# One decoder layer on one core: the order of the attention pairs, feature-turned normed rows, and residual products right behind each norm

## The chip, the cores and the metric

The kernel runs on one core of one Trainium2 chip. The metric is the device time of one execution, in microseconds (us). TensorE (PE) multiplies, VectorE (DVE), ScalarE (ACT) and GpSimd (POOL) do the rest; SyncE (SP), ScalarE and GpSimd also issue DMA transfers. All values are float32. A matmul with float32 operands shows as two records in the trace, so "x8" in a row is four matmuls.

## What is computed

One layer with a prompt of 256 tokens (two tiles of 128) and 8 sample tokens, D = 1024. Shortened:

```python
u, cB, cC, q, k, v, qi, ki, wi, qm, g = split(x @ w_in)     # one projection, 6216 columns
# branch A: short gated convolution; branch C: 4 heads over 256 memory tokens
# branch B: 8 heads; an indexer scores keys, each query keeps k of them
sc  = sum_h relu(qi_h . ki) * wi_h          # prompt: top 64 of 256; samples: top 256 of 2049
p   = softmax(q . k[chosen]);  out = p @ v[chosen]    # samples gather k, v rows from a paged cache
m   = g0*(convA @ w_a) + g1*(attn @ w_b) + g2*(mem @ w_c)
h   = LN(alpha*x + m @ w_o)
# router: best of 4 groups, best 2 of its 8 experts; 32 experts, each 1024 -> 2x256 -> 1024
y   = sum_e gate[:, e] * (silu(a_e) * b_e) @ w_down[e],   a_e, b_e = h @ w_up[e]
out = LN(alpha*h + y)
```

The expert weights are 32 x 3 MiB, read once.

## The kernel before, in words

Each engine has one instruction list, written by hand, with semaphores between them. There is no planner: the order of the source is the order on each engine.

**Start and projections** (PE `chunk`, L563 on). `x` is turned, then `w_in` comes in 1 MB units through four slots. ScalarE issues the loads of the constants (L1327, L1329). A bisection over the sample scores runs beside the gate tiles (`gate_tile`, 24 tiles of 4 x 128 columns of `w_in`, eight matmuls each).

**Attention** (PE L813 to L920). Twelve heads in six pairs: pairs 0 and 1 are memory heads, 2 to 5 are prompt heads. For pair p, `scores(p)` writes two PSUM banks; `softmax(n)` on VectorE scales (and masks) a head's scores into SBUF and takes the row maxima; `exps(n)` on ScalarE; `inverse(n)` on VectorE; `normalise(n)` on ScalarE; `turn(n)` on TensorE turns the probabilities; `values(p)` multiplies them with the values; `head_out(p)` on VectorE copies the result out. Gate tiles stand between these as other work for TensorE. VectorE also has the indexer sums (L2101) and 16 rounds that find the 64 largest scores (`topk_round`, L2055); prompt heads need all of them.

**Samples' keys and values.** When the 256 positions per sample are known (`idx_ready`, L2045), GpSimd issues 16 gathers of key rows (L1632), at most two of them open, then 16 gathers of value rows (L1648), four per pair. Key products are shared out: 12 on GpSimd into four buffers (L1645), each summed on VectorE (`key_sum`, L1845), 5 wholly on VectorE (`key_dot`: L1686 and L1855). Softmax and value product of the samples are interleaved with the branch tiles (`branch_tile`, L895) and their `merge` on VectorE (L2091). SyncE loads `w_o` into the keys' place when all key products are summed (L447), and the first expert weights when the sample values are done (`sa_p`, 9 of them).

**First norm and router** (PE L940 to L1045, DVE L2204 to L2345). `wo_first`, `wo_second` are the output projection (L946, L965). Tile 0, the samples, then tile 1: `residual`, `ln_stats`, `ln_centre` (into `ytmp`), `ln_rstd`, `ln_scale` (into `h3`, `h_ready`). The router's logits come from the un-normed rows. `wo_ps` 4 marks the end of the output projection. `residual_tile(t)` multiplies `h3` by alpha and opens the PSUM banks in which the experts' output is added (L1008, L1012).

**Experts** (PE L1025 to L1260). A token's slot in an expert is a one-hot column of `Ssl`; a gather is a matmul with `h3[:, t, k::KT]` as weights (128 features k, k+8, ...) and `Ssl` moving: `first_part` (L1028), `first_gather` (L1060), `second_gather` (L1079), `gather` (L1097). Eight quads of four experts; SyncE streams their weights in 2 MB units through nine places (`p` counts them), waiting for `used_w` from p = 9 on. Expert 0's lower half comes aside (`down_0`, `down_1`).

## Time and profile before

| | |
|---|---|
| median of 3 runs | 612.38 us (610.49 to 614.92) |
| the profiled execution | 612.95 us, its span 611.1 us |
| PE busy | 551.1 us (90%) |
| PEld busy | 348.4 us (57%) |
| DVE busy | 277.9 us (45%) |
| ACT, POOL busy | 101.1 us, 63.9 us |
| mean granted TensorE clock | 0.954 |
| HBM read | 160.14 MB, 267 GB/s over the span |

The span is the time from the first to the last instruction; the profiled execution's own time is 1.85 us longer. Shares are means over stages with different limits: each stage has to be read by itself, in stretches of time and in the order of each engine.

### The profile page before, as it was taken

How to read it: one execution, taken by the hardware profiler on the slowest of the kernel's cores; microseconds unless marked ns; L12 is line 12 of the kernel's file. 1: busy time of each engine (PE TensorE's matmuls, PEld its weight loads, DVE VectorE, ACT ScalarE, POOL GpSimd, SP SyncE). 2: the span in 40 equal slices, each digit the busy share in tenths (PEclk: the TensorE clock that was granted, in tenths of full speed). 3: DMA queues.
4: the chain of work that ended last, by engine and by line, in shares of the span. 5: the costliest groups of instructions: out<-in, count | busy, mean ns of one | idle time of the engine just before them, and what ended most of it. 6: DMA issues, size and time to landing. Idle time of an engine off the chain costs nothing.

```text
span 611.1 us, 8674 instructions
## 1 busy us (share of the span) xinstructions
PE 551.1 (90%) x3518; PEld 348.4 (57%) x3518; DVE 277.9 (45%) x766; ACT 101.1 (17%) x243; POOL 63.9 (10%) x70
## 2 busy tenths in 40 slices
PE   7999999999999995999799899999999995987671
PEld 4556566475688773777576456766654661522120
DVE  1273765666677687759862496312010200100026
ACT  1001111011310123545100211011101110101011
POOL 0000000000200034587200000000000000000002
PEclk9999999998999996999899997999999999897796
DMA  8981231944443445576869926899999999999971
GB/s 294 372 321 45 93 138 50 365 140 140 131 132 120 139 138 189 175 242 190 330 247 403 321 70 262 306 417 388 424 390 422 420 419 420 422 419 421 417 302 71
DMA packets 47886, 163.53 MB, mean 268 GB/s; under 512 B 5954, under 2 KB 22812, under 8 KB 35812
## 3 DMA queue, kind: packets, MB, share of 16 engines
q1 hardware_dynamic: 39280, 139.81, 59.4%
q0 software_dynamic: 3472, 14.31, 6.9%
q10 hardware_dynamic: 5092, 8.83, 4.0%
q8 instruction: 29, 0.48, 0.3%
q14 instruction: 13, 0.11, 0.1%
HBM read 160.14 MB, written 2.77 MB: 267 GB/s over the span
## 4 chain that ended last, share of the span: by engine, by line
PE 57%; DMA 17%; DVE 17%; ACTq 5%; issue 2%; ACT 1%; SPq 0%; POOLq 0%; POOL 0%; DVEq 0%
PE bank L578 11%; DMA ring<-in_w_down 10%; PE bank L769 10%; PE bank L1122 6%; DMA ring<-in_w_up 5%; PE bank L539 4%; PE bank L1214 2%; PE bank L965 2%; ACTq L1476 2%; PE bank L624 2%; ACTq L1475 2%; DVE ring L1686 2%; PE bank L1079 2%; PE bank L1097 2%; PE bank L592 2%
## 5 line engine op out<-in xcount | busy, mean ns | idle before, releaser
L769 PE MATMUL bank<-work,ring 128*128 128x264 f32 x384 | 94.1, 396 | 0.0
L578 PE MATMUL bank<-ring,work 128*128 128x512 f32 (+2 forms) x224 | 90.6, 544 | 2.1 <-DMA ring<-in_w_in 2.1
L769 PEld LDWEIGHTS bank<-work,ring 128*128 128x128 f32 x384 | 71.2, 192 | 14.8 <-issue 2.8
L1122 PE MATMUL bank<-ring,work 128*32 128x512 f32 x304 | 52.4, 665 | 14.2 <-DMA ring<-in_w_up 11.0
L578 PEld LDWEIGHTS bank<-ring,work 128*128 128x128 f32 x224 | 40.0, 190 | 32.8 <-issue 29.7
L2350 DVE SCALAR_TENSOR_TENSOR work<-work,bank 128x256 f32<-128x256 f32 x8 | 3.4, 422 | 87.0 <-ACT work L1530 87.0
L2362 DVE COPY gates<-bank 128x512 f32<-128x512 f32 x8 | 5.5, 692 | 74.7 <-PE bank L1214 67.7
L895 PE MATMUL bank<-work,ring 128*128 128x264 f32 x128 | 32.6, 400 | 4.3 <-DVE gates L2091 4.3
L1122 PEld LDWEIGHTS bank<-ring,work 128*32 128x32 f32 x304 | 13.9, 121 | 37.5 <-issue 37.4
L1122 PE MATMUL bank<-proj,work 128*32 128x512 f32 x128 | 30.6, 622 | 2.3 <-DMA ring<-in_w_up 1.9
L895 PEld LDWEIGHTS bank<-work,ring 128*128 128x128 f32 x128 | 24.0, 195 | 12.5 <-DVE gates L2091 5.1
L1214 PE MATMUL bank<-ring,work 128*32 128x512 f32 x176 | 27.0, 635 | 2.8 <-DMA ring<-in_w_down 2.1
L1665 POOL TENSOR_TENSOR proj<-proj,ring 128x512 f32<-128x512 f32 x1 | 1.3, 1268 | 255.6 <-ACT proj L1577 255.6
L1157 PE MATMUL bank<-gates,work 128*128 128x512 f32 x56 | 25.4, 596 | 0.0
L1097 PE MATMUL bank<-gates 128*128 128x256 f32 x96 | 24.4, 411 | 0.0
L1351 ACT ACTIVATE work<-bank 128x512 f32<-128x512 f32 x16 | 9.6, 597 | 87.2 <-PE bank L539 87.2
L1097 PEld LDWEIGHTS bank<-gates 128*128 128x128 f32 x96 | 23.2, 335 | 0.1
L1779 DVE SCALAR_TENSOR_TENSOR work<-bank,work 128x512 f32<-128x512 f32 x16 | 11.1, 692 | 25.3 <-PE bank L624 25.2
L1632 POOL DMA_INDIRECT ring<-in_cache_k,idx x16 | 15.3, 955 | 68.4 <-DVE idx L2045 51.6
L1394 ACT ACTIVATE gates<-bank,gates 128x264 f32<-128x264 f32 x24 | 11.5, 480 | 65.1 <-PE bank L769 60.1
L539 PE MATMUL bank<-cst,proj 128*128 128x128 f32 (+1 forms) x80 | 14.5, 304 | 7.5 <-ACT proj L1433 6.9
L624 PEld LDWEIGHTS bank<-work 128*128 128x128 f32 x128 | 16.4, 191 | 8.2 <-issue 8.2
(337 smaller groups left out, 845.1 us busy)
## 6 DMA issues: line engine op xcount, KB each, us to landing
ring<-in_w_up SPq DMA_DIRECT2D x19, 2048.0 KB, 19.8
ring<-in_w_down SPq DMA_DIRECT2D x13, 2048.0 KB, 24.3
ring<-in_w_in SPq DMA_DIRECT2D x22, 1024.0 KB, 5.9
proj<-in_w_up SPq DMA_DIRECT2D x8, 2048.0 KB, 20.7
misc<-in_w_up SPq DMA_DIRECT2D x5, 1024.0 KB, 25.9
gates<-in_w_up SPq DMA_DIRECT2D x5, 1024.0 KB, 20.2
ring<-in_w_o SPq DMA_DIRECT2D x4, 1024.0 KB, 8.7
proj<-in_w_down SPq DMA_DIRECT2D x2, 2048.0 KB, 24.3
```

The costliest lines, as they stand in the source:

```text
L539: return nc.tensor.transpose(out, in_, ident[0:n, 0:n])
L578: last = mm(bank[2 * (i % 2) + t][:, 0:w], lhs[:, k, 128 * t:128 * t + 128], rhs[:, k % 4, :], start=(k == 0), stop=(k == KT - 1))
L592: last = mm(bank[4 + i % 2][32 * j:32 * j + 32, 0:w // 4], lhs[:, k, 256:288], rhs[:, k % 4, j * w // 4:(j + 1) * w // 4], start=(k == 0), ...
L624: last = mm(bank[6][:, 128 * i:128 * i + 128], kt4[g % 2][:, 128 * i:128 * i + 128], QB, start=True, stop=True)
L769: last = mm(b[:, 0:TOK], w[:, k, 128 * (n % 2):128 * (n % 2) + 128], xT[:, k, 0:TOK], start=(k == 0), stop=(k == KT - 1))
L895: last = mm(b[:, 0:TOK], w2[:, k % 2, 128 * n:128 * n + 128], brT[:, k0 + k, 0:TOK], start=(k == 0), stop=(k == nk - 1))
L965: last = mm(bank[2 + dh][:, :], mT[k][:, 128:256], wo(k)[:, 512 * dh:512 * dh + 512], start=(k == 0), stop=(k == 6))
L1097: last = mm(bank[6 + i][:, PC * kk:PC * kk + PC], h3[:, t, k::KT], Ssl[:, t, :], start=(t == 0), stop=(t == 2))
L1122: last = mm(bank[5][32 * j:32 * j + 32, :], xTe[q // 2 % 2][:, k, s0:s0 + CAP], up_of(n + j // 2, j % 2, r), start=(k == 0), stop=(k == KT ...
L1157: mm(bank[2 * t + dh][:, :], GT[q % 2][:, 128 * t:128 * t + 128], Ysb[:, 512 * dh:512 * dh + 512], start=False, stop=False)
L1214: last = mm(bank[6 + dh][32 * j:32 * j + 32, :], hT2[:, f, 32 * j:32 * j + 32], wd, start=(f == 0), stop=(f == 1))
L1632: pool.indirect_dma_start(Kg[:, i, :], None, ck, bass.IndirectOffsetOnAxis(ap=idx_sb[:, i:i + 1], axis=0))\
```

## The change

- **Start**: the big load of constants is issued after the first weight unit has landed, and behind ScalarE's copies of the turned `x`.
- **Pairs**: `scores(0)` and its maxima move ahead of the compaction; memory heads take maxima and exponentials straight from PSUM; `scores(p+1)` stands between the two turns of pair p; all indexer sums stand ahead of the first top-k round; `head_out` moves from VectorE to ScalarE.
- **Samples**: gathers are issued without a limit; all 17 key products are on GpSimd, in place, with the value gathers between and behind them; VectorE sums 4, 4, 5, 3 and 1 rows at a time.
- **Norm**: `ln_scale` stays in `ytmp`; ScalarE copies tile 0 and the samples into `hturn`, which stores a row's features as k x 128 + q for feature 8q + k; tile 1 is written there by VectorE (`ln_scale_turned`), and normed once more into `ytmp`. The residual products read `ytmp` right behind each norm. Gathers load `h3[:, t, 128k:128k+128]`.
- **Stream**: `down_0[1]` waits for `route_ready` two units later, and the count of the fullest expert is taken in bank 5.

```diff
-TOPK_ROUNDS = ((8, 10, 14), (14, 16, 16), ...
+TOPK_ROUNDS = ((0, 3, 8, 11), (11, 16, 16, 16), (16, 16, 16, 16), ...
+KEY_SUMS = ((), (), ((0, 4),), ((4, 8),), ((8, 13),), ((13, 16), (16, 17)))
+        hturn = gate_t[:, 0:3072].rearrange("p (t k q) -> p t q k", t=3, k=KT)
@@ sync
-                    sp.wait_ge(kd_mul, NPROD)
-                    sp.wait_ge(kd_dot, NDOT)
+                    sp.wait_ge(kd_sum, NSUMS)
-                if p == NWS:
+                if p == NWS + 2:
                     sp.wait_ge(route_ready, 1)
@@ tensor
+                elif p == 2:
+                    pe.wait_ge(at_e, 4 * p)
...
             index_scores(0)
+            scores(0)
             gate_tile(11)
...
             for p in range(PAIRS_H):
                 turn(2 * p)
-                turn(2 * p + 1)
                 if p + 1 < PAIRS_H:
                     scores(p + 1)
                 if p == 0:
                     gate_tile(14, part=1)
+                turn(2 * p + 1)
...
-            wo_second(0, (0, 1, 2, 3, 4, 5, 7, 6)).then_inc(wo_ps, 1)
+            wo_second(0, (0, 1, 2, 3, 4))
+            pe.wait_ge(h_ready, 1)
+            pe.wait_ge(aid_ready, 1)
+            residual_tile(0).then_inc(res_ps, 1)
+            wo_second(0, (5, 7, 6)).then_inc(wo_ps, 1)
...
             wo_second(1, range(4))
+            pe.wait_ge(h_ready, 2)
+            residual_samples().then_inc(res_ps, 1)
...
-                        last = mm(bank[6 + b][:, 128 * kk:128 * kk + 128], h3[:, t, 4 * b + kk::KT], Ssl[:, t, 0:128],
+                        last = mm(bank[6 + b][:, 128 * kk:128 * kk + 128], h3[:, t, 128 * (4 * b + kk):128 * (4 * b + kk) + 128], Ssl[:, t, 0:128],
@@ scalar
-            act.wait_ge(x2_in, 16)
-            act.dma_start(cst[:, 128:nconst], a["consts"][:, 128:nconst]).then_inc(cst_in, 16)
...
+            act.wait_ge(unit_sem(0), UC[0])
+            act.dma_start(cst[:, 128:nconst], a["consts"][:, 128:nconst]).then_inc(cst_in, 16)
...
+            def h_copied(n, t, m):
+                act.wait_ge(h_ready, n)
+                act.activation(hturn[0:m, t], ytmp[0:m, :].rearrange("p (q k) -> p q k", k=KT), ACT.Copy).then_inc(hp_ready, 1)
@@ gpsimd
+            for i in range(16):
+                key_gather(i)
+            pool.wait_ge(sa_p, 4)
+            value_gather(0)
+            value_gather(1)
+            pool.wait_ge(qr_sb, 1)
+            pool.wait_ge(knew_in, 32)
+            pool.wait_ge(kg_in, 16 * 16)
+            for i in range(17):
+                key_product(i)
+                if i % 2 == 1 and 2 + i // 2 < 9:
+                    value_gather(2 + i // 2)
+            for i in range(9, 16):
+                value_gather(i)
@@ vector
+            def key_sum(i0, i1):
+                dve.wait_ge(kd_mul, i1)
...
                     inverse(2 * p + 2)
                     if p == PAIRS_H - 2:
                         for i0, i1 in KEY_SUMS[p]:
                             key_sum(i0, i1)
                     inverse(2 * p + 3)
...
+            merge(2)
+            for i0, i1 in KEY_SUMS[PAIRS_H - 1]:
+                key_sum(i0, i1)
+            merge(3)
             sample_max(H, 17, sbias)
...
+            dve.wait_ge(hp_ready, 1)
+            dve.wait_ge(res_ps, 1)
             ln_centre(h3, 2, lng, ytmp)
...
+            ln_scale_turned(ytmp, 1, lnb, hp_ready)
```

TensorE at the head of the pair loop, before: the two turns of pair 0 stand together, ahead of the next scores and of a gate tile and a half.

```order
L769 MATMUL bank<-work,ring 128x264 x8
L539 MATMUL bank<-cst,proj 128x128 x8
L828 MATMUL bank<-misc 128x256 x4
L769 MATMUL bank<-work,ring 128x264 x12
L873 MATMUL bank<-proj 64x256 x4
L769 MATMUL bank<-work,ring 128x264 x8
L539 MATMUL bank<-cst,proj 128x128 x8
L828 MATMUL bank<-work 128x128 x2
```

The same place in the change (L535 are turns, L826 scores, L765 gate tiles, L871 values).

```order
L765 MATMUL bank<-work,ring 128x264 x8
L535 MATMUL bank<-cst,proj 128x128 x4
L826 MATMUL bank<-misc 128x256 x4
L765 MATMUL bank<-work,ring 128x264 x4
L535 MATMUL bank<-cst,proj 128x128 x4
L765 MATMUL bank<-work,ring 128x264 x8
L871 MATMUL bank<-proj 64x256 x4
L765 MATMUL bank<-work,ring 128x264 x8
L535 MATMUL bank<-cst,proj 128x128 x4
L826 MATMUL bank<-work 128x128 x2
```

The second turn now has the next pair's scores and half a gate tile ahead of it, and the scores of pair 2 (L826 from `work`) come between the turns of pair 1.

VectorE from the softmax of the last pair to the first merges (L2091), before: L1845 sums a GpSimd product, L1686 with L1855 are products made on VectorE.

```order
L2073 TENSOR_REDUCE misc<-proj 128x1 x2
L1845 TENSOR_REDUCE gates<-misc 128x8
L2079 RECIPROCAL misc<-misc 128x2
L1845 TENSOR_REDUCE gates<-misc 128x8
L2079 RECIPROCAL misc<-misc 128x2
L1845 TENSOR_REDUCE gates<-proj 128x8
L2085 COPY work<-bank 128x256
L1686 TENSOR_TENSOR ring<-ring,proj 128x512
L1855 TENSOR_REDUCE gates<-ring 128x8
L1686 TENSOR_TENSOR proj<-proj 128x512
L1855 TENSOR_REDUCE gates<-proj 128x8
L2091 SCALAR_TENSOR_TENSOR gates<-gates,bank 128x264 x2
```

The change (L2056 and L2059 softmax, L2065 inverse, L1864 sums over several rows, L2097 merge).

```order
L2056 SCALAR_TENSOR_TENSOR proj<-bank,proj 128x384
L2059 TENSOR_REDUCE misc<-proj 128x1 x2
L2056 SCALAR_TENSOR_TENSOR proj<-bank,proj 128x384
L2059 TENSOR_REDUCE misc<-proj 128x1 x2
L2065 RECIPROCAL misc<-misc 128x2
L1864 TENSOR_REDUCE gates<-ring 128x40
L2065 RECIPROCAL misc<-misc 128x2
L2097 SCALAR_TENSOR_TENSOR gates<-gates,bank 128x264 x3
L1864 TENSOR_REDUCE gates<-ring 128x24
L1864 TENSOR_REDUCE gates<-proj 128x8
L2097 SCALAR_TENSOR_TENSOR gates<-gates,bank 128x264
```

No product is left on VectorE; a sum over five rows (128x40) stands between the two inverses, and sums over three and one row behind the third merge.

TensorE in the output projection of tile 1 (L965 `wo_second`, L977 logits, L999 to L1001 slot counts), before.

```order
L965 MATMUL bank<-ring,gates 128x512 x8
L539 MATMUL bank<-cst,gates 128x8 x8
L989 MATMUL bank<-misc,cst 128x72
L977 MATMUL bank<-proj,work 128x36 x8
L977 MATMUL bank<-proj,work 8x36 x8
L965 MATMUL bank<-ring,gates 128x512 x4
L539 MATMUL bank<-cst,gates 128x128 x4
L965 MATMUL bank<-ring,gates 128x512 x3
L999 MATMUL bank<-proj,cst 128x32
L1000 MATMUL bank<-proj,cst 128x32
L1001 MATMUL bank<-proj,cst 128x32
L965 MATMUL bank<-ring,gates 128x512
```

The change (L963 `wo_second`, L980 and L985 the residual products of tile 0 and of the samples, L975 logits).

```order
L963 MATMUL bank<-ring,gates 128x512 x5
L980 MATMUL bank<-gates,cst 128x512 x2
L963 MATMUL bank<-ring,gates 128x512 x3
L535 MATMUL bank<-cst,gates 128x8 x8
L1003 MATMUL bank<-misc,cst 128x72
L975 MATMUL bank<-proj,work 128x36 x8
L975 MATMUL bank<-proj,work 8x36 x8
L963 MATMUL bank<-ring,gates 128x512 x4
L985 MATMUL bank<-gates,cst 32x256 x4
L535 MATMUL bank<-cst,gates 128x128 x4
```

Both residual products now stand inside the output projection, ahead of its last matmuls and so ahead of `wo_ps` 4.

## Rows read from the trace of the kernel before

**Rows 1.** The chain that ended last, end of the weight stream: start us, us, what.
```profile
527.20 63.45 DMA ring<-in_w_down x2
```

**Rows 2.** SyncE's queue in order of time: start us, us, line, operation.
```profile
311.72 0.88 SPq L471 DMA_DIRECT2D ring<-in_w_up  x2
...
370.83 0.88 SPq L471 DMA_DIRECT2D ring<-in_w_up  x2
...
394.94 0.89 SPq L471 DMA_DIRECT2D ring<-in_w_down  x2
```

**Rows 3.** Stretches: us, busy PE PEld DVE ACT POOL, PEclk, DMA share, GB/s.
```profile
235.00:237.50 2.50, 1.12 (x4) 0.72 (x4) 1.74 (x8) 1.76 (x4) 1.47 (x2) 0.50 0.21 59
...
375.00:377.50 2.50, 2.50 (x5) 1.18 (x5) 1.85 (x11) 0.00 (x0) 0.00 (x0) 0.50 1.02 423
...
390.00:392.50 2.50, 2.50 (x22) 1.64 (x25) 0.50 (x4) 0.60 (x1) 0.00 (x0) 1.00 0.52 216
...
392.50:395.00 2.50, 2.50 (x28) 0.78 (x24) 0.00 (x0) 0.00 (x0) 0.00 (x0) 1.00 0.64 210
...
395.00:397.50 2.50, 2.50 (x28) 0.78 (x24) 0.00 (x0) 0.00 (x0) 0.00 (x0) 1.00 0.62 141
...
450.00:455.00 5.00, 5.00 (x52) 1.43 (x44) 0.00 (x0) 0.00 (x0) 0.00 (x0) 1.00 0.90 324
```

**Rows 4.** TensorE in order of time, attention pairs and branch tiles.
```profile
223.32 1.03 PE L828 MATMUL bank<-misc 64*128 64x256 f32 x8
...
236.08 1.12 PE L539 MATMUL bank<-cst,proj 128*128 128x128 f32 x4 [4.93 <-ACT proj L1433]
...
239.18 1.11 PE L539 MATMUL bank<-cst,proj 128*128 128x128 f32 x4 [1.98 <-ACT proj L1433]
...
240.22 2.08 PE L828 MATMUL bank<-misc 64*128 64x256 f32 x8
...
242.23 6.62 PE L769 MATMUL bank<-work,ring 128*128 128x264 f32 x24
...
283.37 0.82 PE L539 MATMUL bank<-cst,proj 128*128 128x128 f32 x6
...
295.73 2.12 PE L895 MATMUL bank<-work,ring 128*128 128x264 f32 x4 [4.14 <-DVE gates L2091]
...
307.75 3.70 PE L730 MATMUL bank<-ring,work 128*32 128x128 f32 x128 [0.78 <-DVE gates L1686]
```

**Rows 5.** VectorE in order of time, the last two pairs.
```profile
285.28 0.56 DVE L2070 SCALAR_TENSOR_TENSOR proj<-bank,proj 128x384 f32<-128x384 f32 x1
...
291.04 2.01 DVE L1686 TENSOR_TENSOR ring<-ring,proj 128x512 f32<-128x512 f32 x1
...
293.08 0.69 DVE L1855 TENSOR_REDUCE gates<-ring 128x8 f32<-128x512 f32 x1
...
293.80 0.69 DVE L1686 TENSOR_TENSOR proj<-proj 128x512 f32<-128x512 f32 x1
```

**Rows 6.** GpSimd in order of time, gathers and a key product.
```profile
219.77 1.02 POOL L1632 DMA_INDIRECT ring<-in_cache_k,idx  x1 [51.60 <-DVE idx L2045]
...
221.10 0.97 POOL L1632 DMA_INDIRECT ring<-in_cache_k,idx  x1 [0.30 <-issue]
...
250.96 0.95 POOL L1632 DMA_INDIRECT ring<-in_cache_k,idx  x1 [2.01 <-DMA ring<-in_cache_k,idx]
...
285.37 1.28 POOL L1645 TENSOR_TENSOR proj<-ring,proj 128x512 f32<-128x512 f32 x1
```

**Rows 7.** ScalarE in order of time, a plain copy (with a scale).
```profile
341.40 1.91 ACT L1479 ACTIVATE work<-work 128x2048 f32<-128x2048 f32 x1 [38.45 <-issue]
```

**Rows 8.** TensorE in order of time, first slot gather.
```profile
378.58 3.88 PE L1028 MATMUL bank<-gates 128*128 128x128 f32 x16
```

**Rows 9.** By line: weight loads, rows stride 8 words (L1028), adjacent (L1157), min/median/max ns.
```profile
L1028 PEld LDWEIGHTS bank<-gates x48: 312/336/338, 377.7 to 390.2; 128*128 128x128 f32 x48
...
L1157 PEld LDWEIGHTS bank<-gates,work x56: 186/190/208, 428.0 to 579.2; 128*128 128x128 f32 x56
```

**Rows 10.** Start: TensorE's first chunk, ScalarE's constants load.
```profile
10.44 13.97 PE L578 MATMUL bank<-ring,work 128*128 128x512 f32 x32 [2.10 <-DMA ring<-in_w_in]
...
6.57 0.35 ACTq L1329 DMA_DIRECT2D cst<-in_consts  x1
```

More of the change, by code:

```diff
@@ L341, in layer @@
         knew_in, vg_in, xres_in, ln_in = (sem(n) for n in ("knew_in", "vg_in", "xres_in", "ln_in"))
-        kg_in = [sem(f"kg_in{i}") for i in range(2)]
+        kg_in = sem("kg_in")
         ln2_in, lnv_in = sem("ln2_in"), sem("lnv_in")
@@ L978, in logits, with residual_tile, residual_samples @@
                 return last
+            def residual_tile(t):
+                for dh in range(2):
+                    last = mm(bank[2 * t + dh][:, :], alpha_id, ytmp[:, 512 * dh:512 * dh + 512], start=True, stop=False)
+                return last
+            def residual_samples():
+                for j in range(4):
+                    last = mm(bank[4][32 * j:32 * j + 32, 0:256], alpha_id[0:NS, 0:32],
+                              ytmp[0:NS, 256 * j:256 * j + 256], start=True, stop=False)
+                return last
             pe.wait_ge(r_ready, 1)
@@ L1035, in _ @@
             mm(bank[5][:, 64:96], ones[:, 0:128], mask[:, 0:32], start=False, stop=False)
-            mm(bank[5][:, 64:96], ones[:, 0:128], mask[:, 64:96], start=False, stop=True).then_inc(pos_ps, 1)
-            first_part(1, range(4), (0, 2))
+            mm(bank[5][:, 64:96], ones[:, 0:128], mask[:, 64:96], start=False, stop=True)
+            for t in range(3):
+                last = mm(bank[5][:, 96:128], ones[:, 0:128], mask[:, 32 * t:32 * t + 32], start=(t == 0), stop=(t == 2))
+            last.then_inc(pos_ps, 1)
+            pe.wait_ge(hp_ready, 3)
             pe.wait_ge(first_s, 2)
-            pe.wait_ge(h_ready, 3)
             for b in range(2):
                 first_part(b, range(4), (1,)).then_inc(first_ps, 1)
-            for t in range(3):
-                last = mm(bank[3][:, 0:32], ones[:, 0:128], mask[:, 32 * t:32 * t + 32], start=(t == 0), stop=(t == 2))
-            last.then_inc(cnt2_ps, 1)
+            pe.wait_ge(cnt_read, 1)
             def first_gather(i):
@@ L1223, in _ @@
                 up_half(0, b)
+            pe.wait_ge(h_ready, 3)
+            residual_tile(1)
             gate_turn(0)
@@ L1649, in value_gather, with key_product @@
                                         bass.IndirectOffsetOnAxis(ap=idx_sb[:, i:i + 1], axis=0)).then_inc(vg_in, 16)
-            for p in range(1, PAIRS_H - 1):
-                pool.wait_ge(at_t, 2 * p + 1)
-                products, gathers = list(KEY_PRODUCTS[p]), list(VALUE_GATHERS[p])
-                for i in range(4):
-                    value_gather(gathers[i])
-                    if i < len(products):
-                        key_product(products[i])
+            def key_product(i):
+                row = Kg[:, i, :] if i < 16 else knew
+                pool.tensor_tensor(row, row, qrep, ALU.mult).then_inc(kd_mul, 1)
+            for i in range(16):
[12 more added lines that the diff above has]
+                value_gather(i)
             pool.wait_ge(m_ready, KT)
@@ L2096, in _ @@
                 w = 128 * (t + 1)
-                for r in range(*INDEX_ROUNDS[i]):
-                    topk_round(r)
                 dve.wait_ge(is_act, i + 1)
```

275 lines of the change are left out of this document (119 added, 156 removed).

## The prediction, made before the change was run

> **What bounds the kernel now.** I read the page's slices first: TensorE is near 100% busy up to 500 us, the DMA engines are full from 400 us to 590 us. Two limits follow each other, so the chain of waits comes next. Its last long piece is a weight load of the experts that ends at 590.65 us [rows 1], 20 us before the end, and from there on nothing in the change touches the work. So the question is when the weight stream ends. SyncE's queue says what starts it: the first expert weights leave at 311.72 us, behind the samples' values; the places of `w_o` are refilled at 370.83 us, behind `wo_ps` 4; the first place freed by the experts is refilled at 394.94 us [rows 2]. The stretches show how full it is: between 390 and 397.5 us it moved 216, 210 and 141 GB/s instead of about 420, and 324 GB/s at 450 to 455 us [rows 3]. A microsecond counts if it brings 311.72 forward, or `wo_ps` 4 after it, or fills one of those holes. Speed on TensorE behind 400 us counts only through the holes.
>
> Up to 311 us the bound is TensorE, so I looked in its order of time for idle time with a releaser. It waits 4.93 and 1.98 us for normalised probabilities before the two turns of pair 0, and 4.14 us before the third branch tile, for VectorE's first merge [rows 4]. Behind the first two it also runs at the lower of its two clocks: the granted clock is 0.50 at 235 us, 1.2 GHz [rows 3], and scores that took 1.03 us take 2.08 [rows 4].
>
> **The parts and their cost.** *Start.* TensorE waits 2.10 us for the first weight unit, until 10.44 us; the constants' load is issued at 6.57 us and shares the engines with it [rows 10]. Behind the unit instead, it gives back about half of the wait, as two transfers share: -1.1 us (ends 0 and -2.1). The constants are needed only by the first rotary step, after the 13.97 us chunk.
>
> *Pairs 0 and 1.* The normalised probabilities of head 0 now exist before the compaction ends, since its scores, maxima and exponentials stand ahead of it and the copy through VectorE is gone. Turn 0 follows the gate tiles at once. Turn 1 has the next scores and half a tile ahead of it. VectorE then has the indexer sums, 3 top-k rounds, two maxima, 5 rounds, and the inverses: by the same durations as before I get the inverses at 240 us and the turns of pair 1 at 243.4 us, so ScalarE is ready 1 to 2 us early. Both idle times go, 6.9 us. The lower clock goes with them: it cost 0.56 us on each turn (four records in 1.12), 1.05 on the scores, and about 0.9 on the tiles (24 records in 6.62 us, [rows 4]; 5.7 at full speed): 3.0 us. Sum -9.9 us; turn 4 then stands at 253.7 us, where I find `normalise(4)` ready at 253.7: no slack. The other end is that one wait of 4.93 us comes back with its half-speed work: -4.
>
> *Samples.* VectorE loses its 5 products, of which one took 2.01 us, and sums 17 rows at 0.69 us each instead [rows 5]. GpSimd: idle until 219.77 us, then 16 gathers at 1.33 us each, the distance of the two that waited for nothing [rows 6]; all keys there by about 245; 17 products of 1.28 us with 7 value gathers of 1.0 between them, until 277; 7 more gathers until 286.5; landed at 290. The samples' values are due on TensorE at 294.6. Covered, by 4 us. The other end for a gather is 2.08 us, (250.96 - 219.77) / 15, when two are open at most [rows 6]; I take 1.33 since nothing waits now, and keep the other as a rival.
>
> *Branch tiles.* From turn 8 (283.37 us, [rows 4]) to the load that waits for the samples' values (311.72, [rows 2]) were 28.3 us. In the new order: merge 0 at 7.9 us after turn 8 (the five-row sum, 3.4 us, stands before it), branch tile 2 at 8.4, sums of four rows 2.8 us, merge 3 at 13.2, then sample steps and merges by turns, probabilities ready at 20.9, values until 24.9. So -3.4 us. The ends are -5.8 (idle 4.14 and about 1.7 at half speed behind it, nothing new added) and 0. The first expert weights then leave 13.3 us earlier, or 14.4 with the start. The full stretch that follows keeps its length: both what it carries and what waits for it move together.
>
> *Norm.* The residual products of tile 0 (4 records of 512 columns, 0.44 us each by [rows 10], 32 records in 13.97) and of the samples (8 records of 256 columns, at most the 1.03 us of the scores, [rows 4]) now stand before `wo_ps` 4: +2.7 us. No wait is added to it: tile 0 is scaled 1 us before TensorE comes to its product, the samples 5 us before. VectorE waits for ScalarE's turned copy: 1024 elements, 0.96 us by the plain copy of 2048 [rows 7], and 3.7 us are there. Writing with a stride could cost more; up to 3 times it is hidden. The Trainium skill, SBUF — State Buffer, Door 1, says that each access that crosses into another 16-byte line pays a penalty; these writes all do, reads of weights no longer. By that rule ScalarE's and VectorE's turned writes would be slow too; the sum stays, as the cover above holds.
>
> *Gathers.* A weight load with stride 8 words takes 336 ns, an adjacent one 190 [rows 9]. A first gather record took 3.88 / 16 = 0.24 us [rows 8]; adjacent ones of 128 columns should take about 0.14, as the turns do at full speed (6 in 0.82 us, [rows 4]): 48 records give 5 to 6 us. So TensorE frees the first weight places about 6 us earlier relative to the norm, even at the lower clock that stands there (0.50 at 375 us, [rows 3]). But the loads started by `wo_ps` 4 are 7.9 MB, 18.7 us at 420 GB/s: they fill the engines until 21.4 us after the old `wo_ps` 4. The hole is closed, not more. It is worth (204 + 210 + 279) GB/s x 2.5 us = 1.7 MB, 4.1 us, and the dip at 450 us another 96 x 5 = 0.5 MB, 1.1 us [rows 3]: -5.2 us. The rest of the gathers' gain is idle time of TensorE. `down_0[1]` now queues behind two units, so TensorE waits some 6 us before the first `down`; the next refill needed from it is issued 6 us before the stream would run dry.
>
> **Sum.** -1.1 - 9.9 - 3.4 + 2.7 - 5.2 = -16.9 us. Against the profiled execution, 612.95 us, that is 596.0 us. The median of the runs is 0.6 us lower than that execution; I leave that in the range. All good ends together give -20.3 (592.7).
>
> **Rivals.** (1) *The pairs stay bound by VectorE and ScalarE.* `exps`, gate outputs, `normalise` and now `head_out` are one list on ScalarE, and turn 4 has no slack. For: the zero margin. Against: the later pairs showed none of these waits. One old wait back: -4 instead of -9.9, 602 us. Chance 0.12. (2) *Gathers run at 2.08 us.* Then keys are there at 257, products end at 289, the last value rows land at 305 instead of before 294.6: 10.8 us come back, 607 us. For: two open gathers did not go faster, and weight loads share the engines. Against: each waited for a landing. Chance 0.08. (3) *The hole moves instead of closing*: `h_ready` 3 comes behind the count and the slots, its 2 MB unit leaves late, or TensorE's wait for `down_0[1]` reaches the stream. 5.2 us lost, 601 us. Chance 0.13. (4) *Slower: GpSimd's products hold VectorE.* Place: 245 to 277 us, where top-k, softmax and sums now run beside 17 products. A VectorE product beside one took 2.01 us instead of 0.69 [rows 5], 1.32 more, about a GpSimd product of 1.28 [rows 6]. If every product held a VectorE step on the path, 17 x 1.32 = 22.4 us: 618 us; it ends slower than before from 13 such holds on. Against: the softmax step that ran beside a product took its usual 0.56 [rows 5]. The Trainium skill, SBUF — State Buffer, Who interferes with whom, has VectorE steps with two SBUF inputs shut out by GpSimd steps that read SBUF; by it, only the mask step of the top-k is left to be held, 1.3 us. Chance 0.03. (5) *The layout does nothing*, since the stream hides it: then the 5.2 us are at stake again; its chance is in (3)'s.
>
> **How the numbers follow.** Forecast 0.64, between 590 and 600 (592.7 at the good ends, and 3 us on either side for what a walk through four stages may miss); (1) 0.12, (2) 0.08, (3) 0.13, (4) 0.03. The range of 8 in 10 goes from 589, the forecast's lower edge against the median, to 605: it takes in (1) and (3) and leaves (2) and (4) out. A measurement of this kernel tells about 1% (6 us) from no change, so faster means under 606.3: all but (2) and (4), 0.89, and half of (2), which stands on that edge, less 0.03 for two rivals together: 0.90. Within 1%: 0.07. Slower: 0.03.
>
> **What would show it.** Right: no idle time before turns 0 to 5 and a clock of 1.00 from 230 to 250 us; the wait before branch tile 2 under 1 us; the first expert weights at 297 us; `wo_ps` 4 about 12 us earlier than before; DMA above 400 GB/s from there to the end of the stream, which ends at 574 us; LDWEIGHTS of the gathers at 190 ns. Wrong: TensorE waiting for ScalarE at a turn (1); a gap before the samples' values with GpSimd or a DMA as releaser (2); a hole in the DMA share 15 to 25 us behind `wo_ps` 4 (3); VectorE steps of 1.3 us more beside L1659 products (4).

## The result, and the profile after

The changed kernel took 619.39 us (median of 4 runs, 617.20 to 621.76) beside 611.43 us for the kernel before (4 runs, 609.91 to 614.92): ratio 1.0123, 95% interval 1.0064 to 1.0182. The forecast was 596.0 us, 589 to 605, so it missed by 23 us and on the wrong side. The profiled run took 617.2 us, its span is 615.3 us.

Where it went is seen in SyncE's queue, in order of time. These rows answer [rows 2].

```profile
315.48 1.03 SPq L467 DMA_DIRECT2D ring<-in_w_up  x2
...
377.11 0.88 SPq L467 DMA_DIRECT2D ring<-in_w_up  x2
...
393.24 0.89 SPq L467 DMA_DIRECT2D ring<-in_w_down  x2
```

The first expert weights leave 3.8 us later than before, not 14 us earlier. So 18.2 of the 21.2 us by which the profiled run missed the forecast lie ahead of 315 us. TensorE in order of time, for [rows 4] (`<-issue` marks idle time for which the profile shows no releaser, `<-remote` one that it cannot name):

```profile
228.68 0.60 PE L535 MATMUL bank<-cst,proj 128*128 128x128 f32 x4
232.27 1.83 PE L826 MATMUL bank<-misc 64*128 64x256 f32 x8 [2.99 <-issue]
...
236.86 0.60 PE L535 MATMUL bank<-cst,proj 128*128 128x128 f32 x4
...
241.12 0.48 PE L765 MATMUL bank<-work,ring 128*128 128x264 f32 x1 [1.03 <-issue]
...
243.93 3.68 PE L765 MATMUL bank<-work,ring 128*128 128x264 f32 x8 [1.72 <-issue]
...
256.63 1.12 PE L535 MATMUL bank<-cst,proj 128*128 128x128 f32 x4 [3.28 <-ACT proj L1437]
...
271.32 0.55 PE L535 MATMUL bank<-cst,proj 128*128 128x128 f32 x3 [2.80 <-ACT proj L1437]
...
290.94 0.49 PE L535 MATMUL bank<-cst,proj 128*128 128x128 f32 x3
```

Turns 0 and 1 (228.68, 236.86) come earlier than before (236.08, 239.18), and without their old waits. Then gate tile 15 crawls: single matmuls with 1 to 2 us of nothing between them, though the code has no wait inside a tile. A late report cannot explain these gaps, since nothing is waited for there. Turn 2 was forecast at 243.4 us and stands at 256.63, turn 4 at 253.7 and stands at 271.32, and turn 8 is at 290.94 where 283.37 - 1.1 - 9.9 = 272.4 was expected. VectorE and, below it, ScalarE in the same stretch:

```profile
227.66 1.01 DVE L2105 SCALAR_TENSOR_TENSOR proj<-misc,proj 128x256 f32<-128x256 f32 x2 [2.53 <-issue]
232.31 1.01 DVE L2105 SCALAR_TENSOR_TENSOR proj<-misc,proj 128x256 f32<-128x256 f32 x2 [3.65 <-issue]
...
245.50 0.69 DVE L2050 TENSOR_REDUCE misc<-bank 128x2 f32<-128x512 f32 x1 [10.03 <-remote]
```

```profile
231.25 0.48 ACT L1399 ACTIVATE gates<-bank,gates 128x264 f32<-128x264 f32 x1 [2.90 <-remote]
...
244.05 0.60 ACT L1465 ACTIVATE proj<-bank 128x512 f32<-128x512 f32 x1 [11.84 <-remote]
```

The maxima at 245.50 need only the scores that TensorE ended at 234.1, and ScalarE's copy at 244.05 only the transposes that it ended at 229.3. So what TensorE reported reached the others 11 and 15 us late, while what ScalarE reported to TensorE arrived at once (its copy ended at 232.21, the scores above began at 232.27). Below, such idle time in front of an input that was ready is called a stop. GpSimd alone did not stop; it was letting out key gathers, one per 1.25 us, for [rows 6]:

```profile
219.67 0.97 POOL L1650 DMA_INDIRECT ring<-in_cache_k,idx  x1 [0.31 <-issue]
220.94 1.02 POOL L1650 DMA_INDIRECT ring<-in_cache_k,idx  x1 [0.30 <-issue]
...
240.17 0.95 POOL L1654 DMA_INDIRECT ring<-in_cache_v,idx  x1 [0.30 <-issue]
241.43 2.48 POOL L1659 TENSOR_TENSOR ring<-ring,proj 128x512 f32<-128x512 f32 x2 [0.32 <-DMA ring<-in_cache_k,idx]
```

The last line needs all sixteen keys. The last of them was let out at 237.67 us, so it was reported as landed within 3.8 us: what the gathers told GpSimd was not late.

The stretches 220 to 250 us (busy time of PE, PEld, DVE, ACT, POOL; granted clock; DMA share; GB/s) give the time lost and the lower clock that followed:

```profile
220.00:230.00 10.00, 9.28 (x49) 6.77 (x47) 5.16 (x13) 4.54 (x12) 7.57 (x8) 1.00 0.75 223
230.00:240.00 10.00, 6.69 (x26) 4.63 (x26) 2.92 (x11) 0.97 (x2) 7.72 (x8) 0.83 0.92 307
240.00:250.00 10.00, 7.01 (x21) 4.05 (x21) 4.40 (x4) 2.58 (x7) 9.16 (x9) 0.66 0.45 125
```

The next two stages did what was forecast. Turn 8 to the samples' load took 24.5 us (24.9 forecast), and from there to `wo_ps` 4 61.6 us against 59.1 before, +2.5 (+2.7 forecast). From there to the end of the last long load of the chain ([rows 1]) it took 216.1 us against 219.8, -3.7 (-5.2 forecast); that load ends at 593.23 us:

```profile
529.84 63.39 DMA ring<-in_w_down x2
```

### The profile page after: what moved, and what is told of

Its sections match the earlier page's. It is cut to its first block, busy times and chain, and to the rows that moved or that the text cites. A ratio compares the mean times of both kernels' runs of the same rounds, so it can differ in the third digit from the quotient of the medians.

```text
span 615.3 us, 8656 instructions
## 1 busy us (share of the span) xinstructions
PE 538.8 (88%) x3518; PEld 328.8 (53%) x3518; DVE 271.1 (44%) x740; ACT 106.6 (17%) x251; POOL 68.6 (11%) x75
## 4 chain that ended last, share of the span: by engine, by line
PE 51%; DMA 20%; DVE 17%; ACTq 5%; issue 3%; another core or an unknown queue 2%; ACT 1%; SPq 1%; POOLq 0%; POOL 0%; DVEq 0%
PE bank L574 11%; DMA ring<-in_w_down 10%; PE bank L765 10%; PE bank L1127 5%; DMA ring<-in_w_up 5%; PE bank L535 3%; PE bank L1219 3%; DMA proj<-in_w_down 3%; ACTq L1490 2%; PE bank L963 2%; PE bank L620 2%; ACTq L1489 2%; PE bank L588 2%; PE bank L1102 2%; PE bank L1084 2%
## 5 line engine op out<-in xcount | busy, mean ns | idle before, releaser
L765 PE MATMUL bank<-work,ring 128*128 128x264 f32 x384 | 96.4, 400 | 4.0 <-issue 4.0
L765 PEld LDWEIGHTS bank<-work,ring 128*128 128x128 f32 x384 | 72.0, 195 | 19.4 <-issue 8.1
L1127 PE MATMUL bank<-ring,work 128*32 128x512 f32 x304 | 51.3, 650 | 15.0 <-DMA ring<-in_w_up 10.9
L1219 PE MATMUL bank<-ring,work 128*32 128x512 f32 x176 | 30.0, 672 | 2.8 <-DMA ring<-in_w_down 2.1
L893 PE MATMUL bank<-work,ring 128*128 128x264 f32 x128 | 31.8, 392 | 0.5 <-DVE gates L2097 0.5
L1102 PE MATMUL bank<-gates 128*128 128x256 f32 x96 | 21.8, 383 | 0.0
L1399 ACT ACTIVATE gates<-bank,gates 128x264 f32<-128x264 f32 x24 | 11.5, 478 | 54.8 <-PE bank L765 51.8
L620 PEld LDWEIGHTS bank<-work 128*128 128x128 f32 x128 | 16.4, 191 | 8.2 <-issue 8.2
L535 PE MATMUL bank<-cst,proj 128*128 128x128 f32 (+1 forms) x80 | 14.5, 293 | 6.7 <-ACT proj L1437 6.1
L1659 POOL TENSOR_TENSOR ring<-ring,proj 128x512 f32<-128x512 f32 x16 | 20.0, 1276 | 0.4 <-DMA ring<-in_cache_k,idx 0.3
## 6 DMA issues: line engine op xcount, KB each, us to landing
gates<-in_w_up SPq DMA_DIRECT2D x5, 1024.0 KB, 21.2
```

The source lines that it names most:

```text
L535: return nc.tensor.transpose(out, in_, ident[0:n, 0:n])
L620: last = mm(bank[6][:, 128 * i:128 * i + 128], kt4[g % 2][:, 128 * i:128 * i + 128], QB, start=True, stop=True)
L765: last = mm(b[:, 0:TOK], w[:, k, 128 * (n % 2):128 * (n % 2) + 128], xT[:, k, 0:TOK], start=(k == 0), stop=(k == KT - 1))
L893: last = mm(b[:, 0:TOK], w2[:, k % 2, 128 * n:128 * n + 128], brT[:, k0 + k, 0:TOK], start=(k == 0), stop=(k == nk - 1))
L1102: last = mm(bank[6 + i][:, PC * kk:PC * kk + PC], h3[:, t, 128 * k:128 * k + 128], Ssl[:, t, :], start=(t == 0), stop=(t == 2))
L1127: last = mm(bank[5][32 * j:32 * j + 32, :], xTe[q // 2 % 2][:, k, s0:s0 + CAP], up_of(n + j // 2, j % 2, r), start=(k == 0), stop=(k == KT ...
```

## The experiments

A count is used beside the rows: how often the trace shows a transfer raising its semaphore. A complete trace of this program has 2,798 such updates. The changed kernel's first trace had 2,490, and from 220 to 246 us only 99 updates of any kind, where the kernel before had 271; but that trace of the kernel before lacked 70 transfer updates too (2,728), without a stop. Where all updates are in the trace and nothing stops, a chip is called prompt, and choking where the engines stop. Runs were made on five chips (e1 to e4, e5 to e8, e9 to e12, e13 to e16, e17 to e19); each time below stands beside the kernel before on the same chip. e3, the change without its key gathers, gave no time.

**e1 and e2: how many gathers are open.** A gather is open from its issue to its landing. Key gathers of the change let out two at a time (the cut shown), and those of the kernel before let out without a limit.

```diff
+                if i >= 2:
+                    pool.wait_ge(kg_in[i % 2], 16 * (i // 2))
                 pool.indirect_dma_start(Kg[:, i, :], ...)
```

> The changed kernel, with the key gathers let out as before the change: at most two open at a time. Theory A (sixteen open gathers hold back the loading of the engines' next instructions, so that VectorE, ScalarE and TensorE stop between 225 and 245 us): the three stops of VectorE (2.5, 3.7 and 10.0 us) go, turn 8 moves from 290.94 to about 273 us; but the keys are then there at 257 us, the products end at 289 and the last value rows land at 305, so the gap before the samples' values gives about 10 us back: 603 to 608 us. Theory B (VectorE's steps are held by GpSimd's products beside them): no gain, since the products run as before and only later: 617 us or more. Theory C (the new order of the pairs leaves VectorE and ScalarE no room in itself): the stops stay where they are, 615 to 620 us.

> The kernel before with this one edit: its sixteen key gathers are let out at once. Theory A: VectorE, ScalarE and TensorE stop for 10 us or more between 225 and 245 us, as in the changed kernel, and it gets slower by about 10 us: 618 to 625 us. Theories B and C: nothing but the gathers changes, the products come at the same places, so 611 us as before, or a little less.

Measured: e1 611.76 us, ratio 0.998 (0.995 to 1.002), outside what any of the three theories gave; e2 611.84 us, ratio 0.999 (0.995 to 1.003). e1 has no stop, and loses to late values what it gains, the wait before the samples' values being

```profile
303.04 5.59 PE L726 MATMUL bank<-ring,work 128*32 128x128 f32 x128 [5.40 <-DMA ring<-in_cache_v,idx]
```

e2 lets out its gathers without a limit and has no stop either, 367 updates from 220 to 246 us. Theory A in its plain form fell. The two kernels also differ in the number of semaphores that their gathers report on, so that came next.

**e4: four open.** The same edit with four semaphores.

> The changed kernel with at most four key gathers open. Theory A: with four open the gathers still come 1.3 to 1.6 us apart, the keys are there by 245 to 248 us, and an instruction load waits behind four gathers at most instead of sixteen: stops of a few us at most, and 596 to 603 us, less than with two open. If four are enough to keep the gather queue always full, the stops stay and it is 610 to 617 us: then it is not the number open but that the queue never runs empty. Theories B and C: 612 to 618 us.

598.76 us, ratio 0.976 (0.968 to 0.984), no stop, first expert weights at 297.28 us where 297.3 was forecast. It seemed to confirm A. It did not, as e9 shows. Nor was it far from no limit at all: a gather of e9 lands a median of 4.5 us after its issue, and one is let out per 1.25 us, so only about four are open at once there (an estimate from these two numbers), never sixteen.

**e5 and e6: one semaphore or two.** The change with its gathers reporting on two semaphores by turns, and the kernel before, all open, with one.

```diff
-    kg_in = sem("kg_in")
+    kg_in = [sem(f"kg_in{i}") for i in range(2)]
-    ....then_inc(kg_in, 16)
+    ....then_inc(kg_in[i % 2], 16)
```

> The changed kernel, its sixteen key gathers all let out at once as it has them, but telling of their landing on two semaphores by turns, as the kernel before has them, instead of on one. Theory D (sixteen open gathers on one semaphore choke the semaphore updates: in the changed kernel about 5 updates are recorded per us from 222 to 246 us, in the kernel before with all open but two semaphores 15 to 30, and only what TensorE tells arrives late): the stops go, the rate of updates returns to 15 and more per us, 594 to 600 us. Theory A (the number of open gathers counts, whatever they tell on): nothing changes, stops of 10 us, 616 to 621 us.

> The kernel before, its key gathers all let out at once and on one semaphore instead of two. Theory D: the updates fall to about 5 per us from 221 to 245 us, VectorE and ScalarE stop as in the changed kernel, and the time rises from 612 to 618 us or more. Theory A': the stops come only where an instruction load or some other point of the changed program falls into the gathers; then this is 611 to 612 us like the same kernel with two semaphores.

e5 618.65 us, ratio 1.006 (1.003 to 1.009), stops of 11.5 us on VectorE and 14.0 us on ScalarE; e6 623.00 us, ratio 1.017 (1.010 to 1.024). In e6 ScalarE stands still for 13 us in front of a copy whose input TensorE had ready, and turn 0, which waited 4.93 us in [rows 4], waits 14.26:

```profile
242.65 0.60 ACT L1412 ACTIVATE misc<-bank 128x512 f32<-128x512 f32 x1 [13.09 <-remote]
```

```profile
245.55 1.12 PE L539 MATMUL bank<-cst,proj 128*128 128x128 f32 x4 [14.26 <-ACT proj L1433]
```

Theory D is dead by e5. e6 shows the choking in the program before the change as well, so nothing else of the change is needed for it. The loading of instructions, the mechanism that theory A named, does not fit either: no packet of an instruction queue moves from 223 to 245 us in the first trace or from 223 to 243 us in e6, so no stop ended with such a load.

**e7 and e8, on the chip of e5 and e6.** Four open, with the strided weight loads back, and with the down weights asked for first.

```diff
-        mm(..., h3[:, t, 128 * k:128 * k + 128], Ssl..., ...)
+        mm(..., h3[:, t, k::KT], Ssl..., ...)
```

```diff
-                if p == NWS + 2:
+                if p == NWS:
                     sp.wait_ge(route_ready, 1)
```

> The changed kernel with at most four key gathers open, and the gathers of the experts' inputs load their weights with a stride of 8 words again (they read other words than the ones wanted; the number of words is the same). If the turned rows earn what was forecast, the weight loads take 0.34 instead of 0.19 us, TensorE's first place comes free about 5 us later, and a hole of up to 4 us opens in the weight stream: 599 to 603 us against 598.8. If TensorE's speed there is hidden by the weight stream altogether: 598 to 599.5 us.

> The changed kernel with at most four key gathers open, and the second half of the first down weights asked for before the two units of the next experts, as in the kernel before, instead of behind them. TensorE then waits up to 10 us less at the first down. If the weight stream alone sets the end: 597 to 599.5 us, no change from 598.8; if the wait of some 13 us reaches the stream through places freed late (the dip to 333 GB/s at 405 us): 595 to 597.5 us.

e7 619.34 us (613.95, 614.25, 624.43 and 626.78, beside 613.73; without an interval), e8 609.80 us, ratio 0.989 (0.982 to 0.996). Both missed what was expected (599 to 603 and 595 to 599.5), and neither answers its question, because both stop, with at most four gathers open, which e4 had not done. ScalarE in e8:

```profile
240.47 0.60 ACT L1465 ACTIVATE proj<-bank 128x512 f32<-128x512 f32 x1 [6.26 <-remote]
...
247.67 0.60 ACT L1465 ACTIVATE proj<-bank 128x512 f32<-128x512 f32 x1 [6.61 <-remote]
```

All four traces of this chip lack updates (2,470 to 2,548 of 2,798), all three of the chip before had every one. So the chip came under suspicion: theory E.

One pattern stands in all five traces with long stops and was not tested. ScalarE went on 2.9, 3.1 and 2.7 us after GpSimd had let out the last gather of an unbroken series (first trace, e5, e6), and 3.1 and 2.3 us after GpSimd paused within the keys, for 2.16 us in e7 and 1.78 in e8. So it may be the pace of letting out, one gather per 1.25 us, rather than how many are open; no run spaced them otherwise on a choking chip.

**e9 to e12: the same kernels on a third chip.** e9 is the changed kernel, not altered.

> The changed kernel once more, as it is, beside its relatives with fewer gathers open. The first four experiments ran in one session and the next four in another, and only in the second the semaphore updates came at 5 per us and the engines stopped, with four gathers open too. Theory E (the stops hang on the chip that the session has, not on the kernel alone): in a session where the updates come at 15 to 30 per us this is 596 to 600 us; where they come at 5 per us, 617 to 621 us. Theory A (sixteen open gathers always choke the updates): 617 to 621 us with stops of 10 us, whatever the others do.

> The changed kernel with at most four key gathers open, a second time. Theory E: within 1 us of the changed kernel where updates are quick, and 604 to 612 us where they are slow, as the one with the down weights first, 609.8 us, had it. Theory A: 596 to 601 us in every session.

> The kernel before with its key gathers all let out at once, on two semaphores, a second time. Theory E: 611 to 613 us where updates are quick; 621 to 625 us where they are slow, like the same with one semaphore. Theory D (one semaphore is the cause): 611 to 613 us in every session.

> The changed kernel with at most two key gathers open, a second time. Theory E: about 612 us where updates are quick, by the late values; where they are slow also some 612 us, as its gathers are spaced like those of the kernel before. If slow updates hurt with two open as well: 616 us or more.

| | time, us | ratio to before (95%) | updates of 2,798 |
|---|---|---|---|
| e9, the change | 598.95 | 0.977 (0.973 to 0.981) | 2,798 |
| e10, four open | 601.52 | 0.979 (0.975 to 0.983) | 2,798 |
| e11, before with all open | 613.38 | 1.000 (0.997 to 1.003) | 2,798 |
| e12, two open | 612.61 | 0.999 (0.996 to 1.003) | 2,798 |

The change takes 599 us here, 2.3% less than before. A is refuted: gathers let out without a limit and no stop. So is C, since the order of the pairs is the same. Theory E passes as far as it says that the same kernel stops on one visit to a chip and not on another. e10 takes 2.6 us more than e9, where within 1 us was expected. TensorE in e9, to be laid beside the rows of the same kernel above:

```profile
228.65 0.60 PE L535 MATMUL bank<-cst,proj 128*128 128x128 f32 x4
...
232.12 0.60 PE L535 MATMUL bank<-cst,proj 128*128 128x128 f32 x4
...
240.90 0.60 PE L535 MATMUL bank<-cst,proj 128*128 128x128 f32 x4
...
251.80 0.55 PE L535 MATMUL bank<-cst,proj 128*128 128x128 f32 x3 [0.53 <-ACT proj L1437]
```

```profile
271.42 0.49 PE L535 MATMUL bank<-cst,proj 128*128 128x128 f32 x3
...
284.05 1.16 PE L893 MATMUL bank<-work,ring 128*128 128x264 f32 x4 [0.33 <-DVE gates L2097]
291.98 3.70 PE L726 MATMUL bank<-ring,work 128*32 128x128 f32 x128 [1.74 <-DVE gates L1703]
```

The stretches 220 to 250 us of e9, at full clock and with TensorE never idle:

```profile
220.00:230.00 10.00, 10.00 (x57) 7.44 (x55) 6.87 (x19) 6.11 (x15) 7.56 (x9) 1.00 0.75 221
230.00:240.00 10.00, 10.00 (x52) 7.75 (x49) 9.11 (x36) 5.24 (x16) 7.57 (x9) 1.00 0.96 331
240.00:250.00 10.00, 10.00 (x57) 7.64 (x56) 9.17 (x27) 2.91 (x8) 6.89 (x6) 1.00 0.65 214
```

The gathers moved as much as in the first trace (221 and 331 GB/s against 223 and 307), so it is not their data that was slow.

**e13 to e16: a fourth chip.** Besides the change again and two open again, the keys by plain loads of adjacent rows (it leaves out that they are the rows wanted), and products between gathers.

```diff
-   pool.indirect_dma_start(Kg[:, i, :], None, ck, bass.IndirectOffsetOnAxis(...))
+   pool.dma_start(Kg[:, i, :], ck[128 * i:128 * i + 128, :])
```

```diff
             for i in range(16):
                 key_gather(i)          # at most two open
+                if i >= 2:
+                    key_product(i - 2)
```

> The changed kernel a third time. Theory E (the chip decides): 596 to 600 us if the trace records all of some 2,800 semaphore updates that loads and gathers make, 617 to 621 us if it records some 2,500, with stops of 3, 4 and 10 us on VectorE; nothing in between. If it is random from run to run instead, the times on one chip scatter over 20 us.

> At most two key gathers open. Where updates are quick: 611 to 613 us, as twice before, by the values that land 5.4 us late. Where they are slow: if two open are few enough, the same 611 to 613 us, less than the changed kernel; if not, over 616 us.

> The changed kernel with sixteen plain loads of 128 adjacent rows of the keys in place of the sixteen key gathers, issued by GpSimd at the same place, all open (left out: that the rows are those of the pages wanted; bytes and waits are the same). Where updates are slow: if it is the indirect gathers' own way to DRAM that chokes, no stops and 594 to 600 us; if it is any sixteen open transfers, 617 to 621 us. Where updates are quick: 594 to 600 us by either, so it tells nothing.

> The changed kernel with at most two key gathers open and GpSimd's product of a row right behind the issue of the gather two places on, instead of all products behind the last key. The gathers then come about 2.7 us apart, the last key at 262 us, three products and four values behind it until 270, the other twelve values until 286, landed at 289: in time for TensorE at about 292. 597 to 601 us where updates are quick; where they are slow 600 to 606 us, since never more than two keys are open. The rival: products beside VectorE's maxima and small steps from 222 us on hold them by about 1.3 us each; two or three such holds on the way to the turns make 602 to 606 us.

e13 599.42 us, 0.977 (0.974 to 0.981); e14 611.20, 0.998 (0.995 to 1.000); e15 600.51, 0.978 (0.973 to 0.982); e16 607.01, 0.990 (0.987 to 0.993). All updates are in all four traces. Plain loads could tell nothing on such a chip. e16 missed its 597 to 601 and came 1 us above its rival's 602 to 606, whose mechanism, that of rival (4) of the prediction, is seen. Its gathers come slower too. VectorE, and GpSimd below it:

```profile
234.91 1.26 DVE L1713 TENSOR_SCALAR misc<-misc 128x2 f32<-128x2 f32 x1
236.93 1.67 DVE L1713 TENSOR_SCALAR misc<-misc 128x2 f32<-128x2 f32 x1
```

```profile
234.85 1.28 POOL L1661 TENSOR_TENSOR ring<-ring,proj 128x512 f32<-128x512 f32 x1
...
237.28 1.29 POOL L1661 TENSOR_TENSOR ring<-ring,proj 128x512 f32<-128x512 f32 x1
```

A step on two numbers per partition, 0.17 us at 222.30 us in the same kernel, takes 1.26 and 1.67 us beside products, and the mask step at 242.48 takes 2.00. Turn 2 then waits 4.39 us for ScalarE. The Trainium skill, SBUF — State Buffer, Who interferes with whom, lists this kind of step (a tensor with a scalar) among those that can take the port pair that VectorE shares with GpSimd; the trace agrees.

**e17 to e19: a fifth chip.** Two open with products from the tenth key on; the change; the change with strided weight loads as in e7.

> The changed kernel with at most two key gathers open and the products from the tenth key on between the gathers and the values, instead of all behind the last key (e14) or from the third key on (e16). The products then run from about 238 us, behind VectorE's two small steps at 232 us, and the last value rows land at about 289 us. If holds of VectorE's small steps by products were what cost e16 its 8 us: 597 to 601 us where updates are quick. If it was the pace of the gathers: 605 to 608 us as e16. Where updates are slow: 600 to 606 us, because two are open.

> The changed kernel a fourth time. Theory E: 596 to 601 us where the trace records all 2,798 updates of loads and gathers, 617 to 621 us where it records some 2,500.

> The changed kernel with the gathers of the experts' inputs loading their weights with a stride of 8 words again (they read other words than the ones wanted, as many). If the turned rows earn what was forecast: first place free about 5 us later, the hole in the weight stream opens, 599 to 603 us beside a change of 596 to 600 (4 to 5 us more). If the wait of some 16 us for the down weights at 376 us hides it: within 1.5 us of the change.

e17 605.89 us, 0.989 (0.981 to 0.997); e18 597.56, 0.974 (0.968 to 0.979); e19 604.24, 0.985 (0.980 to 0.991). In e17 the small steps take 0.17 us again, but the gathers drew out (the last key is let out at 258.84 us, against 237.48 in e9) and the samples' values wait 4.76 us for the last rows: what was expected if the pace of the gathers costs e16 its time. e19 gives the adjacent weight loads their price (the turned writes stay in it): 6.7 us by the medians, where 4 to 5 was expected. In the traces, `wo_ps` 4 to the end of the stream takes 4.7 us more than in e18 (221.4 and 216.7 us), so about 2 us of it are unexplained. The first 32 records of the first gather, e18 and then e19, and the stretch of the stream, e18 and then e19:

```profile
362.59 5.45 PE L1032 MATMUL bank<-gates 128*128 128x128 f32 x32
```

```profile
360.87 7.89 PE L1032 MATMUL bank<-gates 128*128 128x128 f32 x32
```

```profile
405.00:410.00 5.00, 5.00 (x44) 1.88 (x37) 0.17 (x1) 0.57 (x2) 0.00 (x0) 1.00 0.89 321
```

```profile
405.00:410.00 5.00, 4.48 (x42) 1.70 (x45) 1.27 (x3) 0.38 (x1) 0.00 (x0) 1.00 0.39 159
```

No experiment beats the changed kernel on the same prompt chip: 597.6 to 599.4 us on three chips. The best measured where updates are late is e8, 609.80 us (603.99 to 613.39), with two edits at once.

## Why the prediction was wrong

**The step that failed is *Samples*, "I take 1.33 since nothing waits now"**, together with *Pairs 0 and 1*, which took it for granted that sixteen open gathers cost the other engines nothing. The size of 1.33 us was right, 1.25 were measured. What was missing is a cost to bystanders, put at nothing without a reason. On two of six visits to a chip TensorE's reports reached the others up to 15 us late while gathers were let out, and TensorE itself crawled. The -9.9 us of the pairs became +7.6 + 1.1 = +8.7 (turn 8 against before, 290.94 - 283.37, less the start's forecast -1.1); the difference of 18.6 us is nearly all of the 21.2 us by which the profiled run (617.2) missed 596.0. Neither the trace of before (two gathers open) nor a row on GpSimd could price it, but my bound for sixteen open had an end only above 1.33, for the gathers themselves. It should have had one for the engines beside them. On the three prompt chips the same forecast was within its range (597.6 to 599.4 us), so which chip the first timing fell on was luck, and bad luck here; but no row had excluded it.

**The rest of the sum held in its total**, as e9 shows, whose profiled run took 596.8 us with a span of 594.9. It is the fastest of its four: by medians the gain beside the kernel before is 14.6, 13.5 and 16.4 us on the three prompt chips, against the 16.9 of the sum.

| step | forecast | e9 less before |
|---|---|---|
| start | -1.1 | -1.5 at the first key gather (219.77 to 218.29), within the scatter, see below |
| pairs, turn 8 less the start | -9.9 | 271.42 - 283.37 + 1.5 = -10.5 |
| branch tiles, turn 8 to first expert weights | -3.4 | 24.5 - 28.3 = -3.8 |
| norm, to `wo_ps` 4 | +2.7 | 61.7 - 59.1 = +2.6 |
| holes, `wo_ps` 4 to the end of the stream | -5.2 | 216.8 - 219.8 = -3.0 |
| sum | -16.9 | -16.2 |

These come from e9's queue of SyncE and its chain:

```profile
295.95 1.28 SPq L467 DMA_DIRECT2D ring<-in_w_up  x2
...
357.69 0.88 SPq L467 DMA_DIRECT2D ring<-in_w_up  x2
...
374.80 0.89 SPq L467 DMA_DIRECT2D ring<-in_w_down  x2
```

```profile
540.19 34.32 DMA ring<-in_w_down
```

*Start.* The load behind the unit gave only 0.2 us at the first unit (10.44 to 10.24, idle 1.70 instead of 2.10). The other 1.3 us appear between 106 and 152 us and are not the change's. e2 is the kernel before up to its gathers, and its first one goes out 1.8 us earlier than in [rows 6]; the change itself has it at 218.29 (e9) and at 220.05 (e18). So no gain of the start is shown, and the split of the table is good to about 2 us:

```profile
217.99 1.02 POOL L1630 DMA_INDIRECT ring<-in_cache_k,idx  x1 [51.60 <-DVE idx L2043]
```

```profile
218.29 1.03 POOL L1650 DMA_INDIRECT ring<-in_cache_k,idx  x1 [52.01 <-DVE idx L2090]
```

 *Pairs.* Turn 2 at 240.90 (243.4 forecast), turn 4 at 251.80 (253.7), which waits 0.53 us: the zero margin was real, and rival (1) did not come. *Holes.* The stream was full from 360 to 400 us, so that hole was closed. But the wait for `down_0[1]`, which I put at 6 us, is 8.2, with the stretch

```profile
385.00:390.00 5.00, 0.00 (x0) 0.00 (x0) 0.00 (x0) 0.00 (x0) 0.00 (x0) 0.85 1.01 415
```

without any work, and the stream moves only 372 and 341 GB/s between 400 and 410 us. 2.2 of the 5.2 us did not come. Places freed late by that wait, as in rival (3), would do this; e8, which was to test it, stopped, so it is not shown. *Layout.* The weight loads of the gathers went from 336 to 192 ns (medians), as said with [rows 9]. The 48 records of the first gather take 4.6 us less in e18 than in e19 (2.4 and 2.1 us in its two parts); by its own 0.24 and 0.14 us the prediction should have said 4.8, not 5 to 6. The stream gives 4.7 us back, near the 5.2 that I had at stake. *Turned writes*, bounded in the norm, cost double of what I took (each number goes 128 words behind the one before):

```profile
L1513 ACT ACTIVATE gates<-gates x2: 1957/1980/2004, 340.3 to 347.3; 128x1024 f32<-128x1024 f32 x1, 8x1024 f32<-8x1024 f32 x1
```

```profile
364.78 2.01 DVE L2181 SCALAR_TENSOR_TENSOR gates<-gates,misc,proj 128x1024 f32<-128x1024 f32 x1
```

The copy took 1.98 us instead of 0.96, and VectorE's scaling 2.01 instead of the 1.28 to 1.29 of the same step written straight. Both stayed under their cover, as the bound of three times had it. So the sentence beside the row, slow writes across lines, gave the right sign.

**Rivals.** (4), the one on the slow side, was the right sign for another reason: the small steps at 246.23 and 248.36 us took 1.38 and 2.89 us in the first trace because the stops had pushed them beside the products. Where nothing stops they are over at 233.4 us, before the first product at 243.83. I had left only the mask step to be held; the hold of such small steps, seen in e16, I had not priced. (2), the pace of two open gathers, did not come, but its price was too low: 10.8 us (by its own steps, values 12 us later than at 290 against a need at 294.6, it was 7.4), while two open cost 13.0, 13.7 and 11.8 us beside four or no limit on the same chip (e1 and e4, e12 and e9, e14 and e13).

**Shown, and open.** Shown: the kernel before with its gathers let out without a limit chokes on one chip (e6, on one semaphore, +1.7%) and not on two others (e2, e11, on two; e5 shows that two do not prevent it); the change takes 619 us on one visit and 598 to 599 on three; where the others choke, with two open, the kernel before loses nothing (611.43 and 613.73 us there, 611.65 to 613.93 elsewhere). Not shown: that it is the chip and not the hour, as of the five chips of the experiments none was had twice and the first timing's is not on record; whether the number open or the pace matters; how the change with two open does on a choking chip, as e1, e12 and e14 met prompt ones; and what the bottleneck is. Late reports come only in traces that lack some 9 to 12% of the transfer updates. The Trainium skill, NOTIFIC — the notification-queue block, 7.1 Overflow, says that the block that writes the trace's records can hold back the engine that makes them; if so, the stops belong to the recording, and so may the gaps of TensorE inside gate tile 15, where nothing is waited for. That is the rival that stays open: every time here comes with a recorded span, and no run without one could tell.

## What to carry to other kernels

Price what a quick series of gathers may do to the engines that have nothing to do with them, and give that term an end of its own in the range. When a trace shows engines standing still in front of inputs that were ready long ago, compare when the producer ended with when the consumer began, and count the semaphore updates before blaming the order of the work. And time a surprising kernel on another chip before explaining it: the first four experiments here told a tidy story, of four gathers open instead of sixteen, that the unchanged kernel then refuted. Check a cap against how many are open without it: at 4.5 us each and 1.25 us apart, four hardly binds.

## What was not expected of the hardware

- On two of the six visits to a chip (the first timing, and e5 to e8), ScalarE and VectorE stood for 4 to 14 us in front of what TensorE had ended (11 and 15 us late in the first trace) while gathers were being let out every 1.25 us, and a tenth of the transfers' updates was not in the trace.
- A VectorE step of 0.17 us took up to 2.89 us beside GpSimd's products of 1.28 us, more than two of them.
- A copy with writes 128 words apart cost ScalarE 1.98 us per 1024 elements, where 2048 adjacent ones took 1.91 [rows 7].
- The same program reached its first gather at 217.99 us in one trace and at 219.77 in another (e2 and [rows 6], alike up to there).
